# Gate products of 256 columns, with the high and the low part side by side in the accumulator

## The reference

```python
idx = e1 * PEER_NKEYS + e2
gate = jax.nn.softmax(sc, axis=-1)
h = jax.nn.gelu(jnp.einsum('cd,chkd->chk', xc, u[ic]))
return jnp.einsum('chk,chkd->cd', gc * h, v[ic])
```

## Time and profile before

| | |
|---|---|
| median of three runs | 3307.21 us |
| profiled execution, its own time | 3297.77 us |
| its span | 3296.0 us |
| TensorE busy | 3161.4 us (96%) |
| VectorE busy | 1923.2 us (58%) |
| ScalarE busy | 1490.5 us (45%) |
| mean granted clock of TensorE | 0.979 of full |
| stage with the gates | from 862.7 to 1287.4 us of the span |

### The profile page before, as it was taken

One profiled execution on the slowest core, in us unless ns is written; L12 is line 12 of the kernel. 1 busy time (PEld: TensorE's weight loads), 2 busy tenths in 40 slices (PEclk: granted clock), 3 DMA queues, 4 the chain that ended last, 5 costly groups with the idle time before them and its releaser, 6 DMA issues.

```text
span 3296.0 us, 52600 instructions
## 1 busy us (share of the span) xinstructions
PE 3161.4 (96%) x20572; PEld 2899.5 (88%) x20572; DVE 1923.2 (58%) x2648; ACT 1490.5 (45%) x1977; POOL 3.5 (0%) x10
## 2 busy tenths in 40 slices
PE   6999989999999999999999999699998999999999
PEld 6988779999999999988888888697787999999887
DVE  3456657874666665455555555566565656565444
ACT  2244443444555554444444444434453555555333
POOL 0000000000000000000000000000000000000000
PEclk9899999999999999999999999899999999999999
DMA  7422344556565666676766667333444555554554
GB/s 257 162 71 103 115 142 160 192 195 206 186 212 188 228 227 236 221 242 239 246 239 241 242 237 243 116 141 141 155 178 141 180 188 180 179 185 170 179 192 177
DMA packets 134006, 620.61 MB, mean 188 GB/s; under 512 B 12504, under 2 KB 50330, under 8 KB 67996
## 3 DMA queue, kind: packets, MB, share of 16 engines
q1 hardware_dynamic: 126176, 583.05, 50.8%
q10 hardware_dynamic: 7164, 32.78, 2.6%
q0 software_dynamic: 576, 3.54, 0.3%
HBM read 583.62 MB, written 41.99 MB: 190 GB/s over the span
## 4 chain that ended last, share of the span: by engine, by line
PE 88%; DVE 5%; DMA 2%; ACT 2%; issue 1%; ACTq 0%; DVEq 0%; SPq 0%
PE bank L576 87%; DMA raw<-in_experts_u_t 1%; DVE low L1112 1%; ACT high L1890 1%; DMA raw<-in_w_in_t 1%; DVE act_place L1124 1%; DVE act_low L1128 1%; PE bank L781 0%; ACT big L1908 0%; DMA big<-in_c_onehot_cmp 0%; DVE big L1485 0%; DVE big L1487 0%; DVE big L1482 0%; PE bank L647 0%; DVE big L1439 0%
## 5 line engine op out<-in xcount | busy, mean ns | idle before, releaser
L1112 DVE TENSOR_TENSOR low<-raw,high 128x1024 fp32r<-128x1024 f32 x1008 | 1228.0, 1224 | 1257.2 <-ACT high L1890 1255.5
L1890 ACT ACTIVATE high<-raw 128x1024 fp32r<-128x1024 f32 x1008 | 1060.7, 1058 | 1374.7 <-PE bank L576 1171.5
L576 PE MATMUL bank<-act_high,high 128*128 128x256 f32 x4240 | 1218.4, 287 | 45.6 <-DVE low L1112 21.1
L576 PE MATMUL bank<-act_low,high 128*128 128x256 f32 x4240 | 1206.8, 285 | 0.0
L576 PE MATMUL bank<-act_high,low 128*128 128x256 f32 x4240 | 1206.5, 285 | 0.0
L576 PEld LDWEIGHTS bank<-act_high,high 128*128 128x128 f32 x4240 | 821.2, 194 | 50.1 <-issue 20.1
L576 PEld LDWEIGHTS bank<-act_low,high 128*128 128x128 f32 x4240 | 821.6, 194 | 1.0 <-issue 1.0
L576 PEld LDWEIGHTS bank<-act_high,low 128*128 128x128 f32 x4240 | 820.7, 194 | 0.0
L576 PE MATMUL bank<-high,weighed_high 128*128 128x512 f32 x1024 | 398.5, 389 | 2.1 <-DVE weighed_low L1537 2.1
L576 PE MATMUL bank<-low,weighed_high 128*128 128x512 f32 x1024 | 398.4, 389 | 0.0
L576 PE MATMUL bank<-high,weighed_low 128*128 128x512 f32 x1024 | 398.4, 389 | 0.0
(11 more groups left out here) (224 smaller groups left out, 2227.6 us busy)
## 6 DMA issues: line engine op xcount, KB each, us to landing
raw<-in_experts_u_t SPq DMA_DIRECT2D x128, 1024.0 KB, 5.2
raw<-in_experts_v_t SPq DMA_DIRECT2D x128, 1024.0 KB, 4.9
raw<-in_w_up_t SPq DMA_DIRECT2D x88, 1024.0 KB, 4.8
raw<-in_w_in_t SPq DMA_DIRECT2D x68, 1024.0 KB, 4.9
raw<-in_w_down_t SPq DMA_DIRECT2D x44, 1024.0 KB, 4.8
raw<-in_w_out_t SPq DMA_DIRECT2D x32, 1024.0 KB, 4.8
raw<-in_peer_wq_t SPq DMA_DIRECT2D x16, 1024.0 KB, 4.8
hidden_dram<-big SPq DMA_DIRECT2D x64, 256.0 KB, 5.4
```

Of the source, the lines that this page charges most:

```text
L576: return pe.matmul(out_, lhs_t, rhs, start=start, stop=stop, skip_group_check=True)
L1112: dve.tensor_tensor(low[b][:, :], raw[r][:, HALF * which:HALF * (which + 1)], as_f32(high[b][:, :]), ALU.subtract).then_inc(low_ready[b], 1)
L1890: act.activation(high[b][:, :], raw[r][:, HALF * which:HALF * (which + 1)], ACT.Copy).then_inc(high_ready[b], 1)
```

## The change

- The accumulator space for a slot is two banks, 4 + 2c and 5 + 2c, in place of one. A token has 256 columns in it: 128 for the high part's product and 128 for the low part's.
- `first_high` and `first_low` lie side by side in one buffer `first_both`, so TensorE makes one product of 256 columns per token, with `second` stationary. The parts are not added in the accumulator.
- ScalarE weights all four tokens' high parts; VectorE's instruction for the fourth goes.
- ScalarE copies the high parts' half of the accumulator to `gates_out`, and VectorE adds the low parts' half to it in place (`sum_gates`), after its two `split_low` of the step. TensorE's next use of the slot and ScalarE's store wait for that add (`gates_copied`), and VectorE's add waits for ScalarE's copy (`gates_first`).
- VectorE's one loop becomes four, one for a quarter, as ScalarE's are.

```diff
-ACT_FIRST = 3
...
+        def gate_parts(c):
+            return bank[:, 4 + 2 * c:6 + 2 * c, :].rearrange("p b (u s e) -> p s e (b u)", s=2, e=P)
...
                 for t in range(FOUR):
-                    at = slice(P * t, P * t + P)
-                    mm(bank[:, 6 + c, at], second[:, c, t, :], first_high[:, c, t, :], stop=False)
-                    m = mm(bank[:, 6 + c, at], second[:, c, t, :], first_low[:, c, t, :], start=False)
+                    m = mm(bank[:, 4 + 2 * c + t // 2, 2 * P * (t % 2):2 * P * (t % 2) + 2 * P], second[:, c, t, :],
+                           first_both[:, c, t, :, :].rearrange("p s e -> p (s e)"))
...
-                one = bass.ds(4 * FOUR * n + (FOUR * j + ACT_FIRST), 1)
-                dve.tensor_scalar(first_high[:, c, ACT_FIRST, :], iota[:, :], picked_t[:, 0, one], picked_t[:, 2, one],
-                                  ALU.is_equal, ALU.mult)
...
-            with dve.Fori(0, GATE_QUADS) as n:
-                for j in range(4):
-                    onehots(n, j)
-                    split_tile_low("experts_u_t", n + CHOICE_QUADS, j)
+            def sum_gates(q, n, j):
+
+                c = j % SLOTS
+                at = gates_out[:, q % 2, :, bass.ds(4 * FOUR * n + (FOUR * j - QUARTER * q), FOUR)]
+                dve.wait_ge(gates_first[c], 2 * n + (j // 2 + 1))
+                dve.tensor_tensor(at, at, gate_parts(c)[:, 1], ALU.add).then_inc(gates_copied[c], 1)
+
+            for q in range(T // QUARTER):
+                with dve.Fori(GATE_QUADS // 4 * q, GATE_QUADS // 4 * (q + 1)) as n:
+                    for j in range(4):
+                        onehots(n, j)
+                        split_tile_low("experts_u_t", n + CHOICE_QUADS, j)
+                        sum_gates(q, n, j)
...
-                for t in range(ACT_FIRST):
+                for t in range(FOUR):
                     m = act.activation(first_high[:, c, t, :], first[:, c, t, :], ACT.Copy,
...
-                               bank[:, 6 + c, :].rearrange("p (t e) -> p e t", t=FOUR), ACT.Copy).then_inc(gates_copied[c], 1)
+                               gate_parts(c)[:, 0], ACT.Copy).then_inc(gates_first[c], 1)
```

More of the change, by code:

```diff
@@ L230, in build @@
         onehots_at = big_at + 4 * r3.at
-        second, first, first_high, first_low = [
+        second, first = [
             nc.alloc_sbuf_tensor_at(name, [P, SLOTS, FOUR, P], dt, offset=onehots_at + 4 * n * SLOTS * FOUR * P)
-            for n, (name, dt) in enumerate([("second", F32R), ("first", F32), ("first_high", F32R), ("first_low", F32R)])]
+            for n, (name, dt) in enumerate([("second", F32R), ("first", F32)])]
+        first_both = nc.alloc_sbuf_tensor_at("first_both", [P, SLOTS, FOUR, 2, P], F32R,
+                                             offset=onehots_at + 4 * 2 * SLOTS * FOUR * P)
+        first_high, first_low = first_both[:, :, :, 0, :], first_both[:, :, :, 1, :]
         hidden = Region(BIG - 2 * N).take(2 * N, "p (b n) -> p b n", b=2)
@@ L358, in build @@
         first_high_ready = [sem(f"first_high_ready{c}") for c in range(SLOTS)]
+        gates_first = [sem(f"gates_first{c}") for c in range(SLOTS)]
         gates_done = [sem(f"gates_done{c}") for c in range(SLOTS)]
```

## The result

The changed kernel takes 3317.17 us in the median of seven runs (3311.82 to 3324.38), the kernel before 3307.21 (3298.87 to 3309.61). The ratio is 1.0039, with a 95% interval of 1.0023 to 1.0054: 8 to 18 us slower. The forecast was 3311 us; the time lies inside its range of 3290 to 3329. The profiled executions (3323.15 and 3297.77 us) lie further apart than the medians, and 12 us of that distance stand ahead of the stage, in work that the change doesn't touch: the first gate product starts at 875.0 instead of 862.9. TensorE is busy ahead of it for 804.5 us instead of 793.0, with the same products at a lower mean granted clock (0.95 against 0.96). The other kernels of this study start their gates between 866 and 875. So I compare from the first gate product on.

The account below looks back on a forecast made before the run. TensorE bounds the stage; after the change a ring of copies, one-hots and loads does. TensorE's 26 us go into waits, and the exit adds 3.9 us to the 3307.2 median: 3311 us, range 3290 to 3329.

Parts of the forecast that it names:

- TensorE's step: Gate stage, 64 steps: falls from 6.65 to 6.24 us with wide products, 26 us in all from TensorE alone.
- the ring: Gate stage: two-step loop of copies, subtractions, one-hots and loads becomes the bound, 6.55 us a step.
- late loads: After each quarter's 4 MB gates store a load comes 5.1 us late; spare time no longer repays it.
- turn: Two steps of the ring in the gate stage: from 12.19 to 13.09 us, against TensorE's 12.48.
- The even copy of step 61: ScalarE's copy near the gate stage's end, forecast at 1275.9 us after 29 turns and three quarter ends.
- quarter ends: Three places in the gate stage with late loads: 5.1 us each less 0.15, 14.9 in all.
- exit: End of the gate stage: odd half's copy 3.9 us later, at 1293.1; the stall has no cover, so all shows.
- Same, close to the line: Whole kernel: about 4 us slower, within the 0.2% (6.6 us) that measurement can tell from no change.
- A: Gate stage: TensorE stays the bound, a turn no longer than 12.48 us; 3292 us; chance 0.17.
- B: VectorE's queue: the add is slow through strided access, 0.8 us or more; 3330 us at 1.2; chance 0.18.
- C: Gate products: 4 wide cost what 8 narrow do, step stays 6.65 us; 3316 us; chance 0.15 together with D.
- D: Quarter ends cost more through clock and loop entry, +3 to +6 us; 3315 us; chance 0.15 together with C.

Follow-up runs that it names:

- the add's place: Changed kernel with VectorE's add of a step put behind the next step's one-hots instead of ahead of them: 3301 us, ratio 0.9989.
- the fourth part: Changed kernel with the fourth token's weighted high part made by VectorE again, between its one-hots: 3306 us, ratio 1.0000.
- ScalarE's order: Changed kernel with ScalarE copying the odd half ahead of the weighted parts: 3290 us, ratio 0.9964; with VectorE's add also behind the next one-hots, 3294 us.
- the spare add: Kernel before with one more 128x512 VectorE instruction behind each step's two subtractions, written where nobody reads: 3314 us, ratio 1.0031.
- the cut stores: Changed kernel with each quarter's 4 MB gates store cut into four of 1 MB, spread over the next 16 steps: 3300 us, ratio 0.9976.

## Why the prediction was right

**The mechanism held: TensorE's step, the ring that takes over, and late loads that nothing repays.** TensorE's step fell to 6.24 us as stated. The add had 0.681 us in the mean, and lets the next instruction start after 0.60 (taken: 0.6). The fourth weighted part cost 0.28 to 0.30 (taken: 0.30). The ring became the bound with a turn of 13.15 us against 13.09. The first even copy that closes a turn came 18.6 us after the first gate product (893.68 - 875.04; forecast 881.4 - 862.9 = 18.5). Which part of the ring costs what is shown by the runs that take each out: the add's place 17.9 us, the fourth part 8.4.

**What was off is size, 3.9 us forecast against 8.9 in the profile.** The even copy of step 61 came at 1291.81, 416.8 us after the first gate product; forecast were 413.0 (1275.9 - 862.9). Of these 3.8 us, 0.1 lies in the first turn, 1.7 in the others (29 x 0.06) and 1.9 in the quarter ends: 19.0, 18.9 and 18.3 less 13.15 are 5.9, 5.8 and 5.2, 16.8 in place of 14.9. The quarter ends are the term that I mis-sized most, and in the wrong direction: I had taken 0.15 off the 5.1 measured before, on the ground that the store moves with the add. From the store's issue to the late load's copy the changed kernel has 16.0, 15.9 and 15.3 us, the kernel before 15.0 to 15.1. The late loads themselves took 11.1, 11.0 and 10.4 us from issue to landing, before 10.5, 10.4 and 10.4; why two of the three took longer is not shown. The turn into the exit was 13.29, another 0.2. At the exit the odd half's copy came at 1309.23, 4.13 us after the last even copy (forecast 4.15), and the late load was as dear as before:

```profile
1309.23 1.05 ACT L1901 ACTIVATE high<-raw 128x1024 fp32r<-128x1024 f32 x1
...
1324.98 1.06 ACT L1901 ACTIVATE high<-raw 128x1024 fp32r<-128x1024 f32 x1 [11.90 <-DMA raw<-in_experts_u_t]
```

That is 15.75 us, before 15.72. The wait of TensorE there is 5.9 us instead of 2.7. From the late copy to the first product of the second matrix it is 81.9 us, before 80.9. This last 1.0, which I had left out of the sum, goes with the half clock: 6.8 us at half clock there, before 3.4. That it is the cause is not shown by a run of its own.

**"Same, close to the line"** was the forecast's word, with a chance of 0.4 each for same and slower. The measured ratio of 1.0039 lies with its whole interval above the 0.2% that I had named: by that measure the kernel is slower, not the same. The direction was right and the size too small.

**The rivals.** A (TensorE stays the bound) is out by the 4.5 us of waits for it; it is what the kernels with ScalarE's order do. Its figure, 3292, was for the 0.6 us out of every turn; the run that has just that, the add moved, took 3301. B (a slow add) is out by the row: 0.68 us with both operands strided. C (TensorE gains nothing) is out by the 25.5 us above. D (quarter ends dearer) was a part of the truth: 1.9 us by the loads, and with the exit's 1.0 some 3. VectorE's four loops in place of one show no gap at their entry: where the second loop gives way to the third, the add starts at 1085.58 and the next one-hots at 1086.18.

## What to carry to other kernels

An engine that is idle for a third of the time can set the pace all the same: follow the buffer that it frees through the load and back, and write down the length of that ring beside the bound's step, before work goes into it. When the bound gets faster, first look at what repays late transfers, since slack in the ring is what has been hiding them. The same instruction costs nothing or its full time by its place in the queue, so try the order before giving up the change.

## What the hardware showed

- A product of 128 columns of these operands costs nearly what one of 256 does, 0.11 against 0.12 us, so halving the number of products at the same number of columns takes off 0.41 us a step. What sets the 0.11 is not shown here.
- TensorE's half clock (1.2 instead of 2.4 GHz) followed all three stalls of 1.6 to 1.9 us in the kernel before with the spare add, and none of those of at most 1.2 in the kernel before. In the changed kernel, where the ring is the bound, it came with the 5.3 to 6.1 us stalls too (granted clock 0.77 and 0.74 in the two stretches of 7 us from 991 on), and the turns behind them stayed at 13.0 to 13.3, so no cost of it is seen there. But a stall of that length is not enough to tell: with ScalarE's order the third stall, of 3.59 us at 1195.6, had a granted clock of 1.00 behind it, while the first two (3.53 and 3.60) had 0.50 for 3.4 us; and in the changed kernel with the cut stores a stall of 1.84 us at 1221.5 had 1.00. What decides between them is not shown.
- A 4 MB store beside the 1 MB loads delays one load by 5 to 6 us; as four stores of 1 MB the same bytes cost some 0.6 us each in the mean. This is in the changed kernel's ring; TensorE never waited for them where the ring was shorter than its step.
